# First attention's scores as three products of high and low halves, compressed scores at chunk 37

## The chip, the core and the metric

The kernel runs on one core of a Trainium2 chip. The metric is the device time of one execution in microseconds. The core has a matrix engine (TensorE, PE in the rows; PEld is its loading of weights), a vector engine (VectorE, DVE), an activation engine (ScalarE, ACT), GpSimd (POOL) and SyncE (SP), which here only issues transfers. Each engine works through its own queue in order and waits on semaphores.

## The reference

One decoder layer on 256 tokens of width 2048, all float32. One projection `h @ w_in` of 7704 columns feeds two groups of heads. What the change touches is the scores of the first group: 8 query heads in 2 groups of 4, with compressed, selected and window branches. With 256 tokens the selection and the window keep all past tokens, so both branches are causal attention with their own keys and values.

```python
proj = h @ w_in[l]
...
s = jnp.einsum('bqghd,bngd->bghqn', qc, k_cmp).astype(jnp.float32) * scale
m = cmp_end[None, :] <= t[:, None]
p_cmp = masked_softmax(s, m) * m
o_cmp = jnp.einsum('bghqn,bngd->bqghd', p_cmp.astype(v_cmp.dtype), v_cmp)
...
s = jnp.einsum('bqghd,bgqkd->bghqk', qc, kg).astype(jnp.float32) * scale
p = masked_softmax(s, m)
o_sel = jnp.einsum('bghqk,bgqkd->bqghd', p.astype(vg.dtype), vg)
...
s = jnp.einsum('bqghd,bkgd->bghqk', qc, kwc).astype(jnp.float32) * scale
p = masked_softmax(s, m)
o_win = jnp.einsum('bghqk,bkgd->bqghd', p.astype(vwc.dtype), vwc)
...
o = gc[..., 0:1] * o_cmp + gc[..., 1:2] * o_sel + gc[..., 2:3] * o_win
...
x = x + mixed @ w_out[l]
```

## The kernel before

The weights are a stream of 92 chunks of 128 x 2048 elements, in a fixed order: 60 chunks of the input projection (15 blocks of 512 columns, 4 chunks each), 16 chunks of the first layers that compress keys and values (`ck`, `cv`, 2 at a time among the others up to chunk 39), and 16 chunks of the output projection. All loops run over the chunk number `c`, once on each engine, and what stands in the code for a `c` on one engine stands in that engine's queue in that order. Nothing else sets the order.

A chunk of a projection is split: ACT copies it to `whi` in the type float32r (`split_hi`, L433), DVE subtracts to get `wlo` (`split_lo`, L703), both two such chunks ahead of PE, into 3 buffers. PE multiplies with halves of the activations, also split: high by high, high by low, low by high (L1088 to L1090), 24 products of 512 columns a chunk, 4 k-steps x 2 tiles of 128 tokens x 3. The compressing chunks are 4 float32 products of 32 columns of weights each, and need no split.

Attention runs among the chunks, in units: units 0 to 3 are the first attention (group `u // 2`, branch `1 + u % 2`), units 4 and 5 the second. `UNIT_AT` = 40, 44, 48, 52, 56, 60 is the chunk behind whose products the scores of a unit stand. For unit `u` at chunk `c`:
- PE `scores(u)` behind chunk `c` (L1249): 4 heads, for token tile 0 against 128 keys and for tile 1 against 256, in float32, to the three banks `S`.
- DVE `maxes(u)` and ACT `exps(u)` at `c + 1`, DVE `weights(u)` at `c + 2` (L827 to L834).
- PE `turn_probs(u)` behind chunk `c + 3` (L1266), ACT `take_pT` and DVE `take_pT_lo` (L820) at `c + 4`: high and low halves of the turned probabilities.
- PE `pv_a(u)` behind chunk `c + 4` (L1284 to L1286), three products of halves with 512 moving columns, and where `u` is odd the compressed branch's product (L1296). Unit 4 and 5 have `pv_b` (L1319 to L1321), with 256 moving columns.

The compressed scores `cmp_scores` (L1220, from `qaT` and `kcmpT`, into bank 0 of `S`) stand behind chunk `CMP_SCORES_AT` = 42. One step later DVE masks them, takes the maximum and subtracts it (L978 to L982), ACT takes the exponential at 44 (L650), DVE makes probabilities of it at 45 (L987 to L996), PE turns them behind 46 (L1230), ACT copies them at 47. Rotated queries and keys (`qaT`, `kaT`, `qbT`, `kbT`) are turned by DVE in 16 steps a block (L763), the last of the first attention's (block 4) at chunk 32. `hid` and `vbd` belong to the compressing layers' second half.

## Time and profile before

| what | us |
|---|---|
| runs | 492.05, 493.35, 493.09 (median 493.09) |
| profiled execution, whole | 492.58 |
| its span | 490.8 |
| PE busy | 480.2 |
| PE weight loads busy | 388.8 |
| DVE busy | 357.8 |
| ACT busy | 221.1 |
| POOL busy | 45.7 |

The profiled execution's span is from the first to the last instruction that the profiler saw, and the device time lies 1.8 us above it. Its granted clock of PE is 0.996 of the full one on the mean. In the timelines each product is drawn with its whole duration, longer than the distance to the next, since products are pipelined; the distance from start to start is what one costs. Rows with a count merge instructions of one line that follow one another. A float32 product shows as two instructions, one of the split type as one. Both have `f32` as their type in PE's rows.

### The profile page before, as it was taken

What the parts mean: (1) busy time and instruction counts of PE and PEld (TensorE: products, weight loads), DVE (VectorE), ACT (ScalarE), POOL (GpSimd) and SP (SyncE); (2) the same over time, 40 slices, a digit from 0 to 9 for tenths busy, and PEclk for the clock granted to TensorE, in tenths of its full rate; (3) what the DMA queues carried; (4) which work ended last, traced back from release to release, by engine and by line L of the source; (5) the groups of instructions that cost most, each with busy time, mean ns of one, the idle gap of its engine ahead of it and who ended that gap; (6) DMA issues with size and microseconds to landing.
All of it is one profiled execution on the core that took longest, in us unless ns stands there. A gap on an engine that the chain in (4) does not pass through costs nothing.

```text
span 490.8 us, 6491 instructions
## 1 busy us (share of the span) xinstructions
PE 480.2 (98%) x2554; PEld 388.8 (79%) x2554; DVE 357.8 (73%) x501; ACT 221.1 (45%) x299; POOL 45.7 (9%) x49
## 2 busy tenths in 40 slices
PE   7999999999999999999999999999999999999994
PEld 6878867777777888888888888888888888888883
DVE  4765979368595896999898847488897998444533
ACT  5657423334333365445445454664535443444331
POOL 1002400020201002020020000002000000203050
PEclk9999999999999999999999999999999999999998
DMA  8999958778779434244253425535784454655004
GB/s 275 410 421 419 354 220 315 316 319 308 310 315 391 146 139 160 88 171 172 86 214 130 158 100 183 171 127 206 276 335 171 172 176 180 250 212 210 1 0 172
DMA packets 17725, 107.71 MB, mean 219 GB/s; under 512 B 2208, under 2 KB 2848, under 8 KB 5792
## 3 DMA queue, kind: packets, MB, share of 16 engines
q1 hardware_dynamic: 15968, 103.95, 55.5%
q10 hardware_dynamic: 1728, 3.36, 1.9%
q8 instruction: 20, 0.33, 0.3%
q14 instruction: 9, 0.07, 0.0%
HBM read 105.20 MB, written 2.10 MB: 219 GB/s over the span
## 4 chain that ended last, share of the span: by engine, by line
PE 92%; DMA 4%; DVE 1%; ACT 1%; issue 0%; POOLq 0%; SPq 0%; DVEq 0%; POOL 0%; ACTq 0%
PE acc L1088 27%; PE acc L1090 26%; PE acc L1089 26%; DMA raw<-stream 4%; PE S L1249 3%; PE O L1143 3%; PE S L1266 1%; PE O L1296 1%; PE O L1285 1%; PE O L1286 1%; PE O L1284 1%; DVE wlo L703 0%; ACT whi L433 0%; DVE wlo L726 0%; PE O L1169 0%
## 5 line engine op out<-in xcount | busy, mean ns | idle before, releaser
L703 DVE TENSOR_TENSOR wlo<-raw,whi 128x2048 fp32r<-128x2048 f32 x72 | 165.5, 2303 | 84.2 <-ACT whi L433 83.7
L433 ACT ACTIVATE whi<-raw 128x2048 fp32r<-128x2048 f32 x72 | 137.9, 1917 | 162.0 <-PE acc L1090 149.5
L1088 PE MATMUL acc<-whi,hT_hi 128*128 128x512 f32 x440 | 174.4, 396 | 0.6 <-DVE wlo L703 0.6
L1089 PE MATMUL acc<-wlo,hT_hi 128*128 128x512 f32 x440 | 171.5, 390 | 0.0
L1090 PE MATMUL acc<-whi,hT_lo 128*128 128x512 f32 x440 | 171.4, 390 | 0.0
L1088 PEld LDWEIGHTS acc<-whi,hT_hi 128*128 128x128 f32 x440 | 82.6, 188 | 24.3 <-issue 6.7
L1090 PEld LDWEIGHTS acc<-whi,hT_lo 128*128 128x128 f32 x440 | 82.6, 188 | 17.7
L1089 PEld LDWEIGHTS acc<-wlo,hT_hi 128*128 128x128 f32 x440 | 82.6, 188 | 16.6
L381 POOL TENSOR_TENSOR stage<-stage,stage 128x512 f32<-128x512 f32 (+1 forms) x16 | 23.4, 1476 | 180.9 <-DVE stage L754 180.9
L515 ACT ACTIVATE e<-S,small 128x128 f32<-128x128 f32 (+1 forms) x48 | 19.5, 419 | 26.4 <-DVE small L800 26.4
L763 DVE STREAM_TRANSPOSE zT<-stage 32x256 f32<-32x256 f32 x64 | 27.9, 436 | 2.0
L1088 PE MATMUL acc<-whi,mixA_hi 128*128 128x512 f32 x64 | 24.9, 389 | 0.0
L1089 PE MATMUL acc<-wlo,mixA_hi 128*128 128x512 f32 x64 | 24.9, 389 | 0.0
L1090 PE MATMUL acc<-whi,mixA_lo 128*128 128x512 f32 x64 | 24.9, 389 | 0.0
L1088 PE MATMUL acc<-whi,mixB_hi 128*128 128x512 f32 x60 | 23.3, 389 | 0.0
L1089 PE MATMUL acc<-wlo,mixB_hi 128*128 128x512 f32 x60 | 23.3, 389 | 0.0
L1090 PE MATMUL acc<-whi,mixB_lo 128*128 128x512 f32 x60 | 23.3, 389 | 0.0
L405 POOL TENSOR_TENSOR x_nat<-x_nat,fw 128x512 f32<-128x512 f32 x6 | 11.9, 2003 | 120.9 <-ACT junk L572 120.9
L763 DVE STREAM_TRANSPOSE qaT<-stage 32x256 f32<-32x256 f32 x32 | 14.0, 436 | 3.7 <-POOL stage L381 2.8
L763 DVE STREAM_TRANSPOSE qbT<-stage 32x256 f32<-32x256 f32 x32 | 13.9, 436 | 0.9
L763 DVE STREAM_TRANSPOSE kbT<-stage 32x256 f32<-32x256 f32 x32 | 13.9, 436 | 0.9
L1089 PEld LDWEIGHTS acc<-wlo,mixA_hi 128*128 128x128 f32 x64 | 12.0, 188 | 2.5
(186 smaller groups left out, 487.7 us busy)
## 6 DMA issues: line engine op xcount, KB each, us to landing
raw<-stream SPq DMA_DIRECT2D x72, 1024.0 KB, 4.9
row_raw<-stream SPq DMA_DIRECT2D x16, 1024.0 KB, 6.4
raw<-stream SPq DMA_DIRECT2D x6, 512.0 KB, 9.6
x_nat<-x_rows SPq DMA_DIRECT2D x2, 1024.0 KB, 15.9
x_nat<-x_rows SPq DMA_DIRECT2D x1, 2048.0 KB, 9.3
xTs<-xT SPq DMA_DIRECT2D x3, 512.0 KB, 12.5
raw<-stream SPq DMA_DIRECT2D x4, 256.0 KB, 6.1
fw<-final_w ACTq DMA_DIRECT2D x1, 1024.0 KB, 5.2
```

Source lines behind the costliest of these rows:

```text
L381: pool.tensor_tensor(stage[:, t, 0:w], stage[:, t, 0:w], stage2[:, t, 0:w], ALU.add)\
L405: pool.tensor_tensor(y, y, fw[:, n * NB:(n + 1) * NB], ALU.mult).then_inc(yw_ready, 1)
L433: act.activation(whi[:, n % SPLIT, :], raw[:, n % RAW, :], ACT.Copy).then_inc(hi_ready, 1)
L515: act.activation((e0 if t == 0 else e1)[:, i, :], src, ACT.Exp, bias=nmax[:, 4 * t + i:4 * t + i + 1], accum_out=sums[:, 4 * t + i:4 * t + ...
L703: dve.tensor_tensor(wlo[:, n % SPLIT, :], raw[:, n % RAW, :], whi[:, n % SPLIT, :].bitcast(f32), ALU.subtract)\
L763: dve.transpose(out[:, :, :, SQ * i:SQ * (i + 1)], src[:, :, :, SQ * j:SQ * (j + 1)])\
L1088: pe.matmul(acc_bank(n), xh, wh, start=k == 0, stop=False)
L1089: pe.matmul(acc_bank(n), xh, wl, start=False, stop=False)
L1090: last = pe.matmul(acc_bank(n), xl, wh, start=False, stop=k == KT - 1)
L1143: last = pe.matmul(O[32 * i:32 * (i + 1), k, :], blkf[kind][:, CH * j + i, :, :].rearrange("p g n -> p (g n)"), row_raw[:, m % ROW_RAW, i ...
L1249: last = pe.matmul(dst, q[:, t * P:(t + 1) * P], k[:, 0:w], start=True, stop=True)
L1266: last = pe.transpose(S[:, k, i * P:(i + 1) * P], e[:, i, kt * P:(kt + 1) * P], ident)
```

## The change

- The products of units 0 to 3 are each replaced by three: high by high, high query by low key, low query by high key, all of them float32r. Unit 4 and 5 keep one float32 product.
- The halves are made a group at a time: ACT copies 4 heads of queries (1024 elements a partition) and the group's 2 keys (512) to `q_hi` and `k_hi` (`group_hi`, at c = 38 and 45), DVE subtracts in place to `qa_lo` and `ka_lo` (`group_lo`, at 39 and 46).
- The compressed scores stand behind chunk 37, their mask and shift at 38, their exponential at 39. What follows them stays at 45 to 47.
- `hidT8` moves to another place in memory. Waits are added: unit 0's scores for the mask of the compressed ones and for the low halves, the copy of values of block 9 for the scores of unit 3, the second `hid` for the exponential of the compressed scores, group 1's high halves for the scores of unit 1.

```diff
@@ -75,12 +75,12 @@
 GATE_AT, GATE_TURN = 9, 13
-CMP_SCORES_AT = 42
+CMP_SCORES_AT, CMP_PROBS_AT, HALVES_AT = 37, 45, (38, 45)
 UNIT_AT = [40, 44, 48, 52, 56, 60]
 K_END, V_END = LAST["ck", 0], LAST["cv", 0]
-HID_TURN, KEYS_AT, VALUES_AT = (K_END + 2, CMP_SCORES_AT), K_END + 6, CMP_SCORES_AT + 1
+HID_TURN, KEYS_AT, VALUES_AT = (K_END + 2, V_END + 3), K_END + 6, V_END + 4
 W_PIECES = [(0, i, 1) for i in range(4)] + [(c, i, 2) for c in (1, 2, 3) for i in (0, 2)]
@@ -150,7 +150,9 @@
         hidT = sb("hidT", [P, 4, 2 * NC], at=r1b + 2048)
-        hidT8 = sb("hidT8", [P, 4, 8, NC], at=r1b + 2560)
+        hidT8 = sb("hidT8", [P, 4, 8, NC], at=r1 + 25600)
+        q_hi = sb("q_hi", [P, 4, SEQ], f32r, at=r1 + 16384)
+        k_hi = sb("k_hi", [P, 2, SEQ], f32r, at=r1 + 20480)
         gT = sb("gT", [P, SEQ], at=r1b + 4608)
         kbT = sb("kbT", [P, 8, SEQ], at=r1 + 8192)
@@ -166,6 +168,8 @@
         kaT = sb("kaT", [P, 4, SEQ], at=r2 + 8192)
+        qa_lo = sb("qa_lo", [P, 8, SEQ], f32r, at=r2)
+        ka_lo = sb("ka_lo", [P, 4, SEQ], f32r, at=r2 + 8192)
         va = sb("va_hi", [P, TT, NB], f32r, at=r2 + 12288)
         subw = sb("subw", [P, 2 * HEAD], at=r2 + 15360)
@@ -251,6 +255,7 @@
             sem(n) for n in ("scores_done", "max_ready", "exp_done", "probs_ready"))
+        qk_hi, qk_lo = sem("qk_hi"), sem("qk_lo")
         probs_turned, pT_hi_ready, pT_lo_ready, pv_done, o_taken = (
         cs_done, cs_masked, cs_shift, ce_done, pc_ready, pc_turned, pcT_ready, pc_taken = (
@@ -274,6 +279,10 @@
             return [m[:, t, at] for m in ((va, va_lo) if b == 2 else (vb, vb_lo))]
+
+        def group_keys(m, g):
+
+            return m.rearrange("p (b g) s -> p g b s", g=2)[:, g, :, :]
             kind, b, _ = STREAM[c]
@@ -476,6 +485,8 @@
                 a = use_done(b, t)
+                if b == 9:
+                    act.wait_ge(scores_done, TT * N_A)
                 dst = values(b, t)[0]
@@ -491,6 +502,7 @@
                     act.wait_ge(hid_turned, k)
+                    act.wait_ge(ce_done, 1)
                 act.activation(hid[:, :], O[:, k, :], ACT.Copy).then_inc(hid_taken, 1)
             def silu_hid(k):
@@ -504,6 +516,14 @@
                                        src[:, :, g:g + 1, :].to_broadcast([P, 4, 4, NC]), ACT.Silu).then_inc(hid_act, 1)
+
+            def group_hi(g):
+
+                act.wait_ge(heads_turned, turned(3 + g))
+                if g:
+                    act.wait_ge(scores_done, TT * 2)
+                act.activation(q_hi[:, :, :], qaT[:, 4 * g:4 * g + 4, :], ACT.Copy).then_inc(qk_hi, 1)
+                act.activation(k_hi[:, :, :], group_keys(kaT[:, :, :], g), ACT.Copy).then_inc(qk_hi, 1)
@@ -645,10 +665,13 @@
                     silu_hid(1)
+                for g in range(2):
+                    if c == HALVES_AT[g]:
+                        group_hi(g)
                 if c == CMP_SCORES_AT + 2:
                     act.activation(ce[:, :, :, :], cs[:, :, :, :], ACT.Exp).then_inc(ce_done, 1)
-                if c == CMP_SCORES_AT + 5:
+                if c == CMP_PROBS_AT + 2:
                     act.wait_ge(pc_turned, 1)
                         .then_inc(pcT_ready, 1)
@@ -788,6 +811,15 @@
+            def group_lo(g):
+
+                dve.wait_ge(cs_done, TT)
+                for i, (hi, full, lo) in enumerate(((q_hi[:, :, :], qaT[:, 4 * g:4 * g + 4, :], qa_lo[:, 4 * g:4 * g + 4, :]),
+                                                    (k_hi[:, :, :], group_keys(kaT[:, :, :], g),
+                                                     group_keys(ka_lo[:, :, :], g)))):
+                    dve.wait_ge(qk_hi, 2 * g + i + 1)
+                    dve.tensor_tensor(lo, full, hi.bitcast(f32), ALU.subtract).then_inc(qk_lo, 1)
+
             def maxes(u):
                 for t in range(TT):
@@ -914,6 +946,9 @@
                     turn_z(Z[-1], range(0, 2))
+                for g in range(2):
+                    if c == HALVES_AT[g] + 1:
+                        group_lo(g)
                 if c == VALUES_AT + 1:
                     dve.tensor_tensor(vbd[:, :, :], O[:, 0, P:2 * P].unsqueeze(1).to_broadcast([P, 2, P]),
@@ -981,7 +1016,7 @@
                         .then_inc(cs_shift, 1)
-                if c == CMP_SCORES_AT + 3:
+                if c == CMP_PROBS_AT:
                     cet = ce[:, :, :, :].rearrange("p t h n -> p (t h) n")
                     link(dve.tensor_reduce(cstat[:, 0, :], cet[:, :, 0:N_CMP], AX.X, ALU.add))
@@ -1234,27 +1269,29 @@
                     g, br = unit_a(u)
-                    maps = [(qaT[:, 4 * g + i, :], kaT[:, 2 * (br - 1) + g, :]) for i in range(4)]
+                    kh, kl = k_hi[:, br - 1, :], ka_lo[:, 2 * (br - 1) + g, :]
+                    maps = [((q_hi[:, i, :], kh), (q_hi[:, i, :], kl), (qa_lo[:, 4 * g + i, :], kh)) for i in range(4)]
+                    pe.wait_ge(qk_lo, 2 * (g + 1))
                 else:
-                    maps = [(qbT[:, 4 * m + 2 * (u - N_A) + h, :], kbT[:, 4 * m + 2 * (u - N_A) + h, :])
+                    maps = [((qbT[:, 4 * m + 2 * (u - N_A) + h, :], kbT[:, 4 * m + 2 * (u - N_A) + h, :]),)
                             for m in range(2) for h in range(2)]
                     pe.wait_ge(g_exp, TT)
+                    pe.wait_ge(cs_masked, TT)
                 pe.wait_ge(heads_turned, turned({0: 3, 1: 3, 2: 4, 3: 4}.get(u, 8)))
                     w = (t + 1) * P
-                    for i, (q, k) in enumerate(maps):
+                    for i, terms in enumerate(maps):
                         dst = S[:, 0, i * P:(i + 1) * P] if t == 0 else S[:, 1 + i // 2, (i % 2) * SEQ:(i % 2 + 1) * SEQ]
-                        last = pe.matmul(dst, q[:, t * P:(t + 1) * P], k[:, 0:w], start=True, stop=True)
+                        for n, (q, k) in enumerate(terms):
+                            last = pe.matmul(dst, q[:, t * P:(t + 1) * P], k[:, 0:w], start=n == 0, stop=n == len(terms) - 1)
                     last.then_inc(scores_done, 1)
                 banks_free()
-                if u == 0:
-                    pe.wait_ge(cs_masked, TT)
                 if u == 1:
                 before = sum(8 if v < N_A else 4 for v in range(u))
@@ -1345,7 +1382,7 @@
                     cmp_values()
-                if c == CMP_SCORES_AT + 4:
+                if c == CMP_PROBS_AT + 1:
                     turn_cmp()
                     if c == UNIT_AT[u] + 3:
```

PE behind chunk 37 before (`vblkf` are the two compressing chunks 38 and 39, and behind them stand the products of chunk 40):

```order
L1090 MATMUL acc<-whi,hT_lo 128x512
L1143 MATMUL O<-row_raw,vblkf 32x512 [waits row_in0]
L1143 MATMUL O<-row_raw,vblkf 32x512 x3
L1143 MATMUL O<-row_raw,vblkf 32x512 [waits row_in1]
L1143 MATMUL O<-row_raw,vblkf 32x512 x3
L1088 MATMUL acc<-whi,hT_hi 128x512 [waits acc_read_v,lo_ready,hi_ready]
```

And in the changed kernel:

```order
L1125 MATMUL acc<-whi,hT_lo 128x512
L1255 MATMUL S<-kcmpT,qaT 32x16 [waits heads_turned,kcmp_ready]
L1255 MATMUL S<-kcmpT,qaT 32x16 x63
L1178 MATMUL O<-row_raw,vblkf 32x512 [waits row_in0]
L1178 MATMUL O<-row_raw,vblkf 32x512 x3
L1178 MATMUL O<-row_raw,vblkf 32x512 [waits row_in1]
L1178 MATMUL O<-row_raw,vblkf 32x512 x3
L1123 MATMUL acc<-whi,hT_hi 128x512 [waits acc_read_v,lo_ready,hi_ready]
```

The 64 compressed products stand ahead of the compressing chunks; before, they stand behind chunk 42. Behind chunk 40 each of unit 0's 8 score products became three, with `cs_masked` and `qk_lo` as two more semaphores in the first one's wait.

DVE from the rotation of block 5 (the last `stage` rows) to the scores' maxima of unit 0, before (the first low part is of chunk 42, the second of chunk 43):

```order
L751 SCALAR_TENSOR_TENSOR stage<-acc,const 128x512 [waits heads_turned,acc_done]
L753 SCALAR_TENSOR_TENSOR stage_58<-acc,const 128x4x64
L754 SCALAR_TENSOR_TENSOR stage_58<-acc,const 128x4x64
L703 TENSOR_TENSOR wlo<-raw,whi 128x2048 [waits hi_ready]
L763 STREAM_TRANSPOSE qbT<-stage 32x2x4x32 [waits hid_done,rope_ready]
L763 STREAM_TRANSPOSE qbT<-stage 32x2x4x32 x7
L703 TENSOR_TENSOR wlo<-raw,whi 128x2048 [waits hi_ready]
L799 TENSOR_TENSOR S<-S,const_61 128x512 [waits mask_ready,scores_done]
```

And changed:

```order
L774 SCALAR_TENSOR_TENSOR stage<-acc,const 128x512 [waits heads_turned,acc_done]
L776 SCALAR_TENSOR_TENSOR stage_58<-acc,const 128x4x64
L777 SCALAR_TENSOR_TENSOR stage_58<-acc,const 128x4x64
L1013 TENSOR_TENSOR cs<-S,const 128x128 [waits cs_done]
L1013 TENSOR_TENSOR cs<-S,const 128x128
L1016 TENSOR_REDUCE cstat<-cs 128x16 [waits cs_masked]
L1017 TENSOR_TENSOR cs<-cs,cstat 128x256 [waits vstep]
L821 TENSOR_TENSOR qa_lo<-qaT,q_hi 128x1024 [waits qk_hi,cs_done]
L821 TENSOR_TENSOR ka_lo<-kaT,k_hi 128x2x256 [waits qk_hi]
L726 TENSOR_TENSOR wlo<-raw,whi 128x2048 [waits hi_ready]
L786 STREAM_TRANSPOSE qbT<-stage 32x2x4x32 [waits hid_done,rope_ready]
L786 STREAM_TRANSPOSE qbT<-stage 32x2x4x32 x7
```

The mask and shift of the compressed scores (`cs`) and the two subtractions stand ahead of the low part of chunk 42.

ACT in the same place, before (the second row is the high part of chunk 42):

```order
L433 ACTIVATE whi<-raw 128x2048 [waits chunk_used,raw_in1]
L433 ACTIVATE whi<-raw 128x2048 [waits acc_done,raw_in2]
L494 ACTIVATE hid<-O 128x512 [waits hid_turned,hid_done]
L433 ACTIVATE whi<-raw 128x2048 [waits chunk_used,raw_in3]
L515 ACT_TABLE_LOAD
L515 ACTIVATE e_98,small<-S,small 128x128 [waits max_ready]
```

And changed:

```order
L442 ACTIVATE whi<-raw 128x2048 [waits chunk_used,raw_in1]
L525 ACTIVATE q_hi<-qaT 128x1024 [waits heads_turned]
L526 ACTIVATE k_hi<-kaT 128x512
L673 ACT_TABLE_LOAD
L673 ACTIVATE ce<-cs 128x256 [waits cs_shift]
L442 ACTIVATE whi<-raw 128x2048 [waits acc_done,raw_in2]
L506 ACTIVATE hid<-O 128x512 [waits ce_done,hid_turned,hid_done]
L442 ACTIVATE whi<-raw 128x2048 [waits chunk_used,raw_in3]
L535 ACTIVATE e_102,small<-S,small 128x128 [waits max_ready]
```

The high part of chunk 42 stands behind the two copies and the exponential `ce`, whose table load came from elsewhere: the one ahead of unit 0's exponentials is gone, and one stands now ahead of unit 1's.

DVE from the maxima of unit 1 (`small<-S`) on, before (the low part is of chunk 48, and the rows behind it are the weights of unit 1):

```order
L800 TENSOR_REDUCE small<-S 128x4 [waits vstep]
L763 STREAM_TRANSPOSE kbT<-stage 32x2x4x32 [waits rope_ready]
L763 STREAM_TRANSPOSE kbT<-stage 32x2x4x32 x7
L703 TENSOR_TENSOR wlo<-raw,whi 128x2048 [waits hi_ready]
L827 RECIPROCAL small<-small 128x8 [waits exp_done]
L828 TENSOR_TENSOR small<-small,gate 128x8 [waits vstep]
L834 TENSOR_SCALAR e_98<-e_98,small 128x128 [waits vstep]
L834 TENSOR_SCALAR e_98<-e_98,small 128x128 x3
L834 TENSOR_SCALAR e_99<-e_99,small 128x256 x4
```

And changed:

```order
L832 TENSOR_REDUCE small<-S 128x4 [waits vstep]
L786 STREAM_TRANSPOSE kbT<-stage 32x2x4x32 [waits rope_ready]
L786 STREAM_TRANSPOSE kbT<-stage 32x2x4x32 x7
L821 TENSOR_TENSOR qa_lo<-qaT,q_hi 128x1024 [waits qk_hi,cs_done]
L821 TENSOR_TENSOR ka_lo<-kaT,k_hi 128x2x256 [waits qk_hi]
L726 TENSOR_TENSOR wlo<-raw,whi 128x2048 [waits hi_ready]
L859 RECIPROCAL small<-small 128x8 [waits exp_done]
L860 TENSOR_TENSOR small<-small,gate 128x8 [waits vstep]
L866 TENSOR_SCALAR e_102<-e_102,small 128x128 [waits vstep]
L866 TENSOR_SCALAR e_102<-e_102,small 128x128 x3
L866 TENSOR_SCALAR e_103<-e_103,small 128x256 x4
```

The subtractions of group 1 stand ahead of the low part of chunk 48.

## Rows read from the trace of the kernel before

**Rows 1.** The page: engine busy time (share of the span), and the chain by engine
```profile
PE 480.2 (98%) x2554; PEld 388.8 (79%) x2554; DVE 357.8 (73%) x501; ACT 221.1 (45%) x299; POOL 45.7 (9%) x49
...
PE 92%; DMA 4%; DVE 1%; ACT 1%; issue 0%; POOLq 0%; SPq 0%; DVEq 0%; POOL 0%; ACTq 0%
```

**Rows 2.** Timeline of PE (start us, us, engine, line, work) about unit 0's scores
```profile
164.27 2.78 PE L1249 MATMUL S<-kaT,qaT 128*128 128x128 f32 x16
166.70 0.58 PE L1088 MATMUL acc<-whi,hT_hi 128*128 128x512 f32 x1
167.12 0.40 PE L1089 MATMUL acc<-wlo,hT_hi 128*128 128x512 f32 x1
167.35 0.39 PE L1090 MATMUL acc<-whi,hT_lo 128*128 128x512 f32 x1
```

**Rows 3.** Timeline of PE, products of values in unit 4, 256 moving columns
```profile
306.81 0.28 PE L1319 MATMUL O<-vb_hi,pT_hi 128*128 128x256 f32 x1
306.92 0.28 PE L1320 MATMUL O<-vb_lo,pT_hi 128*128 128x256 f32 x1
...
308.96 1.27 PE L1249 MATMUL S<-kbT,qbT 128*128 128x128 f32 x9
```

**Rows 4.** Groups of PE by form (busy us, mean ns), first attention's scores
```profile
L1249 PE MATMUL S<-kaT,qaT 128*128 128x256 f32 x32 | 7.6, 379 | 0.0
...
L1249 PE MATMUL S<-kaT,qaT 128*128 128x128 f32 x32 | 4.3, 278 | 0.0
```

**Rows 5.** Groups of PE's weight loads by form (busy us, mean ns)
```profile
L1319 PEld LDWEIGHTS O<-vb_hi,pT_hi 128*128 128x128 f32 x12 | 2.3, 191 | 0.1
...
L1143 PEld LDWEIGHTS O<-row_raw,vblkf 128*32 128x32 f32 x64 | 1.9, 109 | 2.9 <-issue 2.9
```

**Rows 6.** Timeline of PE, the compressed scores where they stand before
```profile
178.15 1.33 PE L1220 MATMUL S<-kcmpT,qaT 128*32 128x16 f32 x128
```

**Rows 7.** Timeline of DVE, 158 to 197 us, [idle time before <- released by]
```profile
158.92 2.88 DVE L703 TENSOR_TENSOR wlo<-raw,whi 128x2048 fp32r<-128x2048 f32 x1 [0.63 <-ACT whi L433]
...
178.41 1.92 DVE L834 TENSOR_SCALAR e<-e,small 128x128 f32<-128x128 f32 x8
...
182.46 0.48 DVE L978 TENSOR_TENSOR cs<-S,const 128x128 f32<-128x128 f32 x2
...
183.41 0.42 DVE L982 TENSOR_TENSOR cs<-cs,cstat 128x256 f32<-128x256 f32 x1
...
194.89 2.29 DVE L703 TENSOR_TENSOR wlo<-raw,whi 128x2048 fp32r<-128x2048 f32 x1 [2.67 <-ACT whi L433]
```

**Rows 8.** Timeline of ACT, 151 to 201 us
```profile
151.53 1.92 ACT L433 ACTIVATE whi<-raw 128x2048 fp32r<-128x2048 f32 x1 [5.64 <-PE acc L1090]
156.97 1.92 ACT L433 ACTIVATE whi<-raw 128x2048 fp32r<-128x2048 f32 x1 [3.52 <-PE acc L1090]
...
200.35 0.37 ACT L515 ACTIVATE e<-S,small 128x128 f32<-128x128 f32 x1 [5.49 <-DVE small L800]
```

**Rows 9.** Timeline of DVE, 205 to 236 us
```profile
205.98 2.29 DVE L703 TENSOR_TENSOR wlo<-raw,whi 128x2048 fp32r<-128x2048 f32 x1 [0.20 <-ACT whi L433]
...
208.63 1.92 DVE L834 TENSOR_SCALAR e<-e,small 128x128 f32<-128x128 f32 x8
...
219.06 1.87 DVE L820 TENSOR_TENSOR pT_lo<-S,pT_hi 128x512 fp32r<-128x512 f32 x3
...
235.04 2.29 DVE L703 TENSOR_TENSOR wlo<-raw,whi 128x2048 fp32r<-128x2048 f32 x1 [2.18 <-ACT whi L433]
```

**Rows 10.** Timeline of PE, unit 0's and unit 1's transposes, scores and first value product
```profile
185.88 1.47 PE L1266 MATMUL S<-const,e 128*128 128x128 f32 x12
...
194.72 2.78 PE L1249 MATMUL S<-kaT,qaT 128*128 128x128 f32 x16
...
213.94 1.47 PE L1266 MATMUL S<-const,e 128*128 128x128 f32 x12
...
220.78 0.39 PE L1284 MATMUL O<-pT_hi,va_hi 128*128 128x512 f32 x1
```

## The prediction

> **What bounds the kernel now.** I read the page first: TensorE (PE) is busy for 98% of the span and holds 92% of the chain that ended last, nearly all of it in the three product lines [rows 1]. So a microsecond more or less on PE counts in full, and work on VectorE (DVE) or ScalarE (ACT) counts only where it makes PE wait. Three questions follow, each with its own view: what a score product takes on PE (timeline of PE), how late DVE and ACT may be before PE stands (their timelines beside PE's), and where the delay is caught up.
>
> **PE: the score products.** A unit of the first attention has 8 float32 products, 4 with 128 moving columns and 4 with 256; each shows as two instructions (64 in the trace for four units [rows 4]). In unit 0 they start at 164.27. The product behind them is drawn early and long, so I count back from the one after it, at 167.12, less one pitch of 0.23: 166.89. A unit takes 2.62 us [rows 2], for 4 x (128 + 256) = 1536 columns 1.71 ns a column, four times the 0.43 ns of one pass (below). The other three units are drawn alike.
> The change puts 24 products of high and low halves there: 12 of 256 columns and 12 of 128. For 256 columns there is an exact row: 18 such products run from 306.81 to 308.96, 0.119 each [rows 3]; 12 of them are 1.43 us. For 128 moving columns of this type the trace shows nothing, so the cost is bounded:
> - From below by the slope. 512 columns take 0.23 (167.12 to 167.35 [rows 2]), 256 take 0.119: 0.43 ns a column, so 0.064 for 128. A unit would be 12 x 0.064 + 1.43 = 2.20 us, 0.42 less than now.
> - By the weights. Every product here loads 128 columns of weights anew. A load of 128 columns is drawn at 191 ns and one of 32 at 109 [rows 5], 82 ns for 96 columns, so 128 columns need about 0.109 us of loading however few columns move. The nearest row of the same type has a pitch of 0.119 [rows 3], of which 256 x 0.43 = 0.110 would be the stream alone. With 0.109 a unit is 2.74 us, with 0.119 it is 2.86 us.
> - From above by the rate of float32: 128 columns at 1.71 ns are 0.219, if a narrow moving operand of this type falls back to four passes. A unit would be 4.06 us, 1.44 more than now.
> I take 0.109 to 0.119, since a load of new weights stands before each product and one pass per product is what both other widths of this type show. So a unit takes 0.12 to 0.24 us more, not less, and four take **+0.5 to +1.0**. The saving of a quarter in passes is eaten by the loads: three loads a product instead of two.
> The Trainium skill, TensorE: Matmul & The Clock Gate, section LDWEIGHTS, gives columns divided by 1.2 per ns, 107 ns for 128; by that rule, with which the slope of rows 5 agrees, the sum is the same. Its section Back-to-back issue gap gives about 56 ns for 128 columns where weights don't bind; by that a unit would be 2.10 us and the four would save 2.1. No row here shows such a product.
>
> **PE: compressed scores moved.** 128 instructions of 16 columns take some 1.2 us (1.33 drawn with the last one's end [rows 6]). They go from behind chunk 42 to behind chunk 37, on the same engine, still ahead of everything that reads them: 0 on PE. Their inputs (heads, compressed keys) are turned by chunk 32. The moved block on DVE (mask, maximum, shift) starts at 182.46 and ends at 183.83, 1.4 us, 0.1 of it overlap [rows 7].
>
> **Group 0's halves (chunks 38 to 40).** ACT gets a copy of 1024 and one of 512 elements: 2048 take 1.92 [rows 8], so about 1.5 for both, in the idle time between its work of 151.53 to 153.45 and that of 156.97. DVE gets a subtraction of 1024 and one of 512. 2048 elements take 2.29 (205.98) and 512 about 0.62 (three in 1.87 [rows 9]); between them lie some 1.15 for 1024, 1.75 in all. Their start waits for the shift block. DVE is done with its rotation at 158.29, which is 158.92 less the 0.63 of idle time [rows 7]; the shift block takes it to 159.6, the halves to 161.4. Scores of unit 0 come at 164.27 plus the 1.2 moved ahead of them, 165.5: the halves hide with 4 us to spare. ACT's exponential of the compressed scores now stands ahead of the split of chunk 42, which so starts near 160.0 instead of 156.97; DVE's low part of it ends near 164.2 instead of 161.8. PE wants it a chunk after unit 0's scores, near 173: hidden. Transposes, maxima and weights of unit 0 come about 1.7 later; the weights end at 180.33 before [rows 7], so near 182, and PE turns the probabilities at 185.88 [rows 10]. Hidden. The old place of the shift block gives 1.3 back, and an idle time of 2.67 us ahead of 194.89 [rows 7] takes the rest. So group 0: **0**.
>
> **Group 1's halves (chunks 45 to 46).** ACT's two copies and a table load fall between the end of unit 1's scores (194.72 + 2.62 = 197.3 [rows 10]) and the first exponential at 200.35 [rows 8], whose table was loaded earlier before: 1.5 and 1.3 for the load against 3.0 us, hidden within 0.1. DVE's 1.75 us stand ahead of the low part of chunk 48, which had waited 0.20 [rows 9]: 1.55 of delay. Behind it without idle time are the weights of unit 1, transposes, another low part, the rotation of block 7 and the three low parts of the turned probabilities.
> - The weights end at 210.55; 212.1 then, against PE's turn at 213.94 [rows 9, 10]. Hidden by 1.8.
> - The first low part of the probabilities ends at 219.06 + 0.67 = 219.73, and PE takes it at 220.78 [rows 9, 10]: 1.05 us to spare. With 1.55 of delay PE stands 0.50. The chain on both sides starts from chunk 43 on PE, with one score unit between, so that unit's 0.12 to 0.24 comes off: a stall of 0.25 to 0.4, **+0.3**.
> Later units aren't touched: DVE waits for ACT 2.18 us ahead of 235.04 [rows 9], which absorbs the rest.
> The wait of unit 0 for the masked scores, of the values of block 9 and of the second hidden layer name things done long before; PE's and ACT's queues behind them don't wait.
>
> **Sum.** +0.5 to +1.0 and +0.3, together about +1.0 us. On the profiled execution's own time of 492.58 (span 490.8 and 1.8 around it) that is 493.6; that execution lies 0.5 below the median of the runs, so the forecast on the median of 493.09 is **494.1**. A measurement of this kernel can tell about 0.3% (1.5 us) from no change.
>
> **Rivals.**
> - *Narrow products run at the float32 rate* (the other side, clearly slower). Four times 1.44 is +5.8; PE is then so late at unit 1 that the stall is gone: 498.9. It decides from about 0.13 us per product of 128 columns: there 48 of them, with the 256-column ones, cost 1.4 over the old scores, and 0.1 of stall. For it: the type is stored in 4 bytes like float32, and no product of it in the trace has fewer than 256 moving columns. Against it: 512 and 256 columns lie on one straight line of a single pass.
> - *Loads hide entirely*, 0.064 for 128 columns. The four units save 1.7, but PE then reaches the probabilities of unit 1 0.4 earlier and stands 0.9: net -0.8, 492.3. For it: loads overlap products everywhere. Against it: their slope per column [rows 5]. With the 56 ns of the skill's page named above the units save 2.1 and the stall is near 1.0: 492.0; the page's rule and this rival are the same mechanism, and they share a chance.
> - *The stall is larger*: if ACT's table load and copies push the exponentials of unit 1, or the strided subtraction of the keys is slower than a flat one, by some 1 us, PE stands 1.3 instead of 0.3: 495.1.
> - *The change doesn't do what it says* (the products stay as they were): only the moves and the stall are left, +0.5, 493.6. I give it nothing of its own, since the types are changed in the code.
>
> **How the numbers follow.** My sum 0.48, narrow products at the float32 rate 0.32, loads hidden 0.13, larger stall 0.07. Faster by over 0.3% means under 491.6: only the hidden loads with no stall, 0.05. Slower means over 494.6: the float32 rate, the larger stall, and a sixth of my own case, 0.45. The rest, 0.50, is within 0.3%. The range must reach to the float32 rate, or it leaves out a third: 492.0 to 499.3. The likeliest case alone goes from 493.4 to 494.9.
>
> **What would show it.** Right: the 24 products of a unit take 2.7 to 2.9 us from the first to the next chunk; 256-column ones at 0.119 pitch; PE idle 0.2 to 0.5 us ahead of unit 1's values, released by DVE's low part; no idle time at units 0, 2 and 3. A pitch of 0.22 at 128 columns means the first rival, one of 0.07 the second. Wrong altogether: PE waiting ahead of unit 0's scores, or for a low part of weights after chunk 46.

## The result, and the profile after

| kernel | median, us | runs | profiled whole | span |
|---|---|---|---|---|
| before, beside it | 492.58 (491.97 to 493.35) | 8 | 492.58 | 490.8 |
| changed | 494.89 (493.81 to 495.28) | 8 | 495.08 | 493.2 |

The ratio is 1.0042, with a 95% interval from 1.0032 to 1.0053: 2.1 us slower. It is taken over all runs of both kernels and is not the quotient of the two medians, which lie 2.3 us apart. Runs of one kernel lie 1.4 us apart and more (before: 491.97 to 493.35; in a later group 491.66 to 494.60), so here and below a median can move by half a microsecond and more where the ratio does not. Measured once more beside the last experiment it was 494.92 against 492.97, 1.0038 [1.0024, 1.0051]. The forecast was 494.1, 1.0 us above the median of 493.09 that was known then, with 0.50 on "within 0.3%" and 0.45 on "slower by over 0.3%". So the sign and the range held, but the size was twice what the sum said, and the case with the larger chance was not the one that came. That 494.89 is only 0.8 above the forecast is in part luck: the kernel before, run beside it, had a median 0.5 below 493.09.

The page of the changed kernel, which answers to [rows 1]: busy time of each engine, and the chain that ended last by engine.

```profile
PE 482.0 (98%) x2586; PEld 391.4 (79%) x2586; DVE 361.2 (73%) x505; ACT 224.2 (45%) x303; POOL 45.7 (9%) x49
...
PE 91%; DVE 4%; issue 1%; DMA 1%; ACT 1%; POOLq 0%; DVEq 0%; SPq 0%; POOL 0%; ACTq 0%
```

PE's share of the chain lost a point and DVE's rose from 1% to 4%. So somewhere the chain leaves PE for DVE. How long PE waited there the share does not say: followed back in time, the chain enters DVE at 220.07 and stays in its queue, which had next to no idle time, back to 195.45, while PE was busy beside it. The length of the wait is read from PE's own rows. The timeline of PE (start, us, engine, line, work) about unit 0's scores first, as [rows 2]:

```profile
165.82 0.22 PE L1288 MATMUL S<-k_hi,q_hi 128*128 128x128 f32 x1
165.88 0.28 PE L1288 MATMUL S<-ka_lo,q_hi 128*128 128x128 f32 x1
165.99 0.27 PE L1288 MATMUL S<-k_hi,qa_lo 128*128 128x128 f32 x1
166.10 0.27 PE L1288 MATMUL S<-k_hi,q_hi 128*128 128x128 f32 x1
...
167.28 0.28 PE L1288 MATMUL S<-ka_lo,q_hi 128*128 128x256 f32 x1
167.40 0.28 PE L1288 MATMUL S<-k_hi,qa_lo 128*128 128x256 f32 x1
...
168.60 0.40 PE L1123 MATMUL acc<-whi,hT_hi 128*128 128x512 f32 x1
```

The distance from one start to the next is called the pitch. It is 0.11 us for products of 128 moving columns and 0.12 for those of 256, and the unit takes 168.60 - 165.82 = 2.78 us. The eight float32 products of before took 2.62: 0.16 more a unit, 0.65 for four.

Then the place of the one new stall in PE's timeline that DVE ends (another, of 1.0 us at the start of the program, is in both kernels). Chunk 48's first token tile ends here, and its second begins:

```profile
218.30 0.39 PE L1124 MATMUL acc<-wlo,hT_hi 128*128 128x512 f32 x1
218.53 0.39 PE L1125 MATMUL acc<-whi,hT_lo 128*128 128x512 f32 x1
220.07 0.50 PE L1123 MATMUL acc<-whi,hT_hi 128*128 128x512 f32 x1 [1.16 <-DVE stage L777]
220.41 0.40 PE L1124 MATMUL acc<-wlo,hT_hi 128*128 128x512 f32 x1
```

From 218.53 to 220.07 are 1.54 us where 0.23 is the pitch, and the next step takes 0.34 instead of 0.23: 1.42 us are lost, and the releaser is not `pT_lo` but L777, the last of three operations that rotate a token tile of a finished block. DVE in the changed kernel, as [rows 9]:

```profile
206.38 1.23 DVE L821 TENSOR_TENSOR qa_lo<-qaT,q_hi 128x1024 fp32r<-128x1024 f32 x1
207.52 0.69 DVE L821 TENSOR_TENSOR ka_lo<-kaT,k_hi 128x512 fp32r<-128x512 f32 x1
208.12 2.29 DVE L726 TENSOR_TENSOR wlo<-raw,whi 128x2048 fp32r<-128x2048 f32 x1
...
216.47 2.29 DVE L726 TENSOR_TENSOR wlo<-raw,whi 128x2048 fp32r<-128x2048 f32 x1
218.68 0.68 DVE L774 SCALAR_TENSOR_TENSOR stage<-acc,const 128x512 f32<-128x512 f32 x1
219.28 0.41 DVE L776 SCALAR_TENSOR_TENSOR stage<-acc,const 128x256 f32<-128x256 f32 x1
219.61 0.41 DVE L777 SCALAR_TENSOR_TENSOR stage<-acc,const 128x256 f32<-128x256 f32 x1
...
221.20 1.87 DVE L852 TENSOR_TENSOR pT_lo<-S,pT_hi 128x512 fp32r<-128x512 f32 x3
```

The low part of chunk 48 starts at 208.12 instead of 205.98, and all that follows is 2.14 later. The first rotated tile is ready at 219.61 + 0.41 = 220.02, and PE goes on at 220.07. The second token tile of block 8 accumulates in the bank in which block 7's first tile was kept, and DVE must have read it. The same two places in the trace of before, which stand in no group above, DVE first and then PE:

```profile
217.47 0.41 DVE L754 SCALAR_TENSOR_TENSOR stage<-acc,const 128x256 f32<-128x256 f32 x1
```

```profile
217.80 0.39 PE L1090 MATMUL acc<-whi,hT_lo 128*128 128x512 f32 x1
218.03 0.41 PE L1088 MATMUL acc<-whi,hT_hi 128*128 128x512 f32 x1
```

There DVE let go of the bank at 217.88, and PE wanted it at 218.03. The reserve was 0.15 us, and no wait shows it.

That this accounts for the whole is read from a stretch, from the start of unit 1's transposes to the start of unit 2's scores. Before, the transposes start at 213.94 [rows 10] and the scores at

```profile
224.36 2.89 PE L1249 MATMUL S<-kaT,qaT 128*128 128x128 f32 x16
```

In the changed kernel:

```profile
214.68 1.47 PE L1303 MATMUL S<-const,e 128*128 128x128 f32 x12
...
226.51 0.33 PE L1288 MATMUL S<-k_hi,q_hi 128*128 128x128 f32 x1
```

PE took 10.42 us before and takes 11.83, 1.41 more. With the 0.65 of the products that is 2.06 us, a ratio of 1.0042 on 492.6.

### The profile page after: what moved, and what is told of

It reads as the page before. It is cut to its first block, busy times and chain, and to the rows that moved or that the text cites. A ratio compares the mean times of both kernels' runs of the same rounds, so it can differ in the third digit from the quotient of the medians.

```text
span 493.2 us, 6572 instructions
## 1 busy us (share of the span) xinstructions
PE 482.0 (98%) x2586; PEld 391.4 (79%) x2586; DVE 361.2 (73%) x505; ACT 224.2 (45%) x303; POOL 45.7 (9%) x49
## 4 chain that ended last, share of the span: by engine, by line
PE 91%; DVE 4%; issue 1%; DMA 1%; ACT 1%; POOLq 0%; DVEq 0%; SPq 0%; POOL 0%; ACTq 0%
PE acc L1123 25%; PE acc L1124 25%; PE acc L1125 25%; PE O L1178 3%; PE S L1288 3%; DVE kbT L786 1%; PE acc L1159 1%; PE acc L1166 1%; PE acc L1162 1%; PE S L1303 1%; DMA raw<-stream 1%; DVE wlo L726 1%; PE O L1333 1%; PE O L1322 0%; PE O L1321 0%
## 5 line engine op out<-in xcount | busy, mean ns | idle before, releaser
L1123 PEld LDWEIGHTS acc<-whi,mixA_hi 128*128 128x128 f32 x64 | 12.0, 188 | 2.5
```

The lines of the kernel that those rows point to most:

```text
L1123: pe.matmul(acc_bank(n), xh, wh, start=k == 0, stop=False)
```

## The experiments

Whole times scatter by about 1 us for a reason that lies outside the change, in the first part of the program: two executions of one and the same kernel (`e4_keys_early` and its repeat) start unit 0's scores at 165.75 and 164.80. The middle doesn't scatter: where a kernel was profiled twice, its stretches agree within 0.06 us. So beside each ratio I give starts of PE's rows from the profiled execution: **the middle stretch** (unit 1's transposes to unit 2's scores) and **S1 to S5** (start of unit 1's scores to start of unit 5's). To S1 to S5 the table adds the change of unit 0's own scores; "ratio from it" is 1 plus that sum over 492.6.

| kernel | middle stretch | S1 to S5 | against before, with unit 0 | ratio from it | ratio measured |
|---|---|---|---|---|---|
| before | 10.42 | 114.24 | | | |
| changed | 11.83 | 116.14 | 1.90 + 0.16 | 1.0042 | 1.0042 |
| changed, second time | 11.89 | 116.19 | 1.95 + 0.16 | 1.0043 | 1.0038 |
| moves alone | 10.46 | 114.28 | 0.04 | 1.0001 | 0.9991 |
| group 1's lows late | 10.39 | 114.69 | 0.45 + 0.16 | 1.0012 | 1.0010 |
| halves made, not used | 12.00 | 115.80 | 1.56 | 1.0032 | 1.0037 |
| only query low late | 10.74 | 115.04 | 0.80 + 0.16 | 1.0019 | 1.0035 |
| the same, repeated | 10.71 | 115.01 | 0.77 + 0.16 | 1.0019 | 1.0031 |
| rotation first | 11.07 | 115.36 | 1.12 + 0.16 | 1.0026 | 1.0026 |
| mixed | 10.72 | 113.67 | -0.57 - 0.29 | 0.9983 | 0.9977 |
| mixed, rotation first | 10.38 | 113.35 | -0.89 - 0.29 | 0.9976 | 0.9976 |

### Moves alone: `e1_moves`

```diff
-                for g in range(2):
-                    if c == HALVES_AT[g]:
-                        group_hi(g)
...
-                for g in range(2):
-                    if c == HALVES_AT[g] + 1:
-                        group_lo(g)
...
-                    maps = [((q_hi[:, i, :], kh), (q_hi[:, i, :], kl), (qa_lo[:, 4 * g + i, :], kh)) for i in range(4)]
-                    pe.wait_ge(qk_lo, 2 * (g + 1))
+                    maps = [((qaT[:, 4 * g + i, :], kaT[:, 2 * (br - 1) + g, :]),) for i in range(4)]
```

> Only the moves of the change: compressed scores behind chunk 37, their mask at 38, their exponential at 39; no halves of queries and keys are made and units 0 to 3 keep one float32 product each. Theory A (the +2.3 us are 4 x 0.16 for the products and 1.4 for a stall of PE ahead of the second token tile of chunk 48, where DVE's rotation of block 7 comes too late because group 1's halves stand ahead of it): ratio to the kernel before 1.000, within 0.3 us. Rival B (the moves themselves cost, since unit 0's scores and the exponentials' table load now wait for other things): +0.5 us or more, ratio above 1.001.

492.32 against 492.83 (12 runs), ratio 0.9991 [0.9979, 1.0003], S1 to S5 within 0.04 us of before. The compressed scores five chunks sooner cost nothing and bring nothing.

### Group 1's low halves behind the probabilities: `e2_late`

```diff
-                for g in range(2):
-                    if c == HALVES_AT[g] + 1:
-                        group_lo(g)
+                if c == HALVES_AT[0] + 1:
+                    group_lo(0)
...
+                if c == UNIT_AT[1] + 4:
+                    group_lo(1)
```

> The changed kernel with one edit: DVE makes group 1's low halves behind the low parts of unit 1's turned probabilities (chunk 48) instead of ahead of the low part of chunk 48's weights. Theory A: DVE's rotation of block 7 is back in time, PE doesn't stand at chunk 48, unit 2's scores find their halves ready by about 1.5 us; left are the products, 4 x 0.16 = +0.65 us over the kernel before (ratio 1.0013). Rival C (DVE's 1.75 us only move the stall, to unit 2's scores or the maxima behind them): +1.5 to +2.3 us stay, ratio 1.003 to 1.005.

492.89 against 492.83, ratio 1.0010 [0.9998, 1.0021]. The same products, the same halves, only 1.74 us of DVE's work (206.38 to 208.12 in the changed kernel) in another place, and the middle stretch is 10.39: the whole stall is gone. PE at the token tile where it stood:

```profile
216.93 0.40 PE L1126 MATMUL acc<-whi,hT_lo 128*128 128x512 f32 x1
217.16 0.39 PE L1124 MATMUL acc<-whi,hT_hi 128*128 128x512 f32 x1
217.39 0.39 PE L1125 MATMUL acc<-wlo,hT_hi 128*128 128x512 f32 x1
```

The row at 217.16 is the first of a k-step, and it follows like any other. What stays by the table is 0.61 us, the products.

### Halves made, products as before: `e3_halves_only`

The subtractions write over the high halves here (an edit in `group_lo` that is left out below), and nothing reads the result. The scores are the float32 products of before.

```diff
-                    maps = [((q_hi[:, i, :], kh), (q_hi[:, i, :], kl), (qa_lo[:, 4 * g + i, :], kh)) for i in range(4)]
+                    maps = [((qaT[:, 4 * g + i, :], kaT[:, 2 * (br - 1) + g, :]),) for i in range(4)]
```

> The changed kernel with the old products: the halves of queries and keys are made at the same places (the low ones written over the high ones, so that the full ones stay), but units 0 to 3 take one float32 product each. Nothing reads the halves. Theory A: the stall at chunk 48's second tile is there without any new product, 1.5 us (0.16 more than in the changed kernel, since PE gets there 0.16 sooner), ratio 1.0030. Rival D (the new products make most of the loss, the stall is a coincidence of the profiled run): +0.5 us or less, ratio up to 1.001.

494.73 against 492.83, ratio 1.0037 [1.0025, 1.0049]. PE behind chunk 48's first token tile:

```profile
218.97 0.50 PE L1124 MATMUL acc<-whi,hT_hi 128*128 128x512 f32 x1 [1.33 <-DVE stage L778]
```

The stall comes without a single changed product, and it is 0.17 us longer (1.33 instead of 1.16 of idle time, 12.00 instead of 11.83). That is what a unit of the older products is shorter: PE comes to the bank earlier by that much and waits longer.

### Only the query subtraction late: `e4_keys_early`, `e4b_keys_early`

```diff
-                        group_lo(g)
+                        group_lo(g, (1,) if g else (0, 1))
...
+                if c == UNIT_AT[1] + 4:
+                    group_lo(1, (0,))
```

> The changed kernel with only the subtraction of group 1's queries (1.13 us start to start) moved behind unit 1's low parts; that of its keys (0.6 us) stays ahead of the low part of chunk 48. Theory A, in which the stall is DVE's delay less what it had to spare, about 0.2 to 0.3 us: PE stands about 0.3 at chunk 48's second tile instead of 1.4, total +0.65 + 0.3 = +0.95 us, ratio 1.0019. If the stall is set by something else than the length of DVE's work (a threshold), it stays at 1.4 or is gone: ratio 1.0042 or 1.0013.

> The kernel of the run with group 1's key subtraction alone in its early place, once more, since its profile and its timed runs did not agree: in the profile the stretch from unit 1's turned probabilities to unit 2's scores was 0.32 us longer than before (as expected), which with the products makes +1.0 us, but the timed runs lay 1.8 us above those of the kernel before. If the profile's stretches are the whole of it, the ratio is 1.0019 to 1.0025; if something that the middle of the trace doesn't show belongs to this kernel, it stays at 1.0035.

494.71 against 492.83, 1.0035 [1.0023, 1.0048]; the repeat 494.16 against 492.22, 1.0031 [1.0021, 1.0042]. The place at issue did as expected: 0.61 us of subtraction (start to start) are left in front, less DVE's 0.20 of idle time [rows 9], less 0.16 by which the unit's products bring PE later, less the reserve of 0.15, plus 0.05 from the release to PE's start and 0.11 for the slower step behind a stall, are 0.26, and the stretch is 0.32 and 0.29 longer. PE in the repeat:

```profile
217.51 0.39 PE L1129 MATMUL acc<-whi,hT_lo 128*128 128x512 f32 x1
217.93 0.50 PE L1127 MATMUL acc<-whi,hT_hi 128*128 128x512 f32 x1
```

0.42 where 0.23 is the pitch: a loss of 0.19 that has no idle time printed beside it, which is why distances from start to start are the safer reading. But the whole was 0.6 to 0.8 us above what this place and the products give, both times, and the interval excludes 1.0019 both times. The excess sits at the very end. The last transfer of a result in the repeat, and in before:

```profile
487.29 0.35 ACTq L710 DMA_DIRECT2D result<-x_nat  x1
```

```profile
486.98 0.35 ACTq L687 DMA_DIRECT2D result<-x_nat  x1
```

The spans end at 491.9 and at 490.8, so 4.6 us behind the issue instead of 3.8. The transfer itself is what took longer: from issue to landing

```profile
result<-x_nat ACTq DMA_DIRECT2D x1, 512.0 KB, 4.2
```

in both profiles of this kernel, and 3.3 or 3.4 in before and in every other kernel here. One more packet of instructions was fetched in both profiles (10, elsewhere 9). No run changes that alone, so whether it is the cause stays open.

### The rotation first: `e7_rope_first`

```diff
+                if c == LAST["in", 7]:
+                    take(c, 0)
...
-                take(c, 0)
+                if c != LAST["in", 7]:
+                    take(c, 0)
```

> The changed kernel with one edit on DVE: at chunk 47 the rotation of block 7's first token tile stands ahead of the low part of chunk 49's weights instead of behind it. Theory A (PE at chunk 48 waits for that rotation and nothing else): the stall of 1.4 us there is gone; the same DVE work still stands ahead of unit 1's low parts of the probabilities, so the stall that the prediction named comes out behind it, 0.3 to 0.4 us ahead of unit 1's value products. Total +0.65 + 0.35 = +1.0 us over the kernel before, ratio 1.0020. Rival C (the delay of DVE costs its 1.4 us in whatever place it comes out): ratio 1.0042 as in the changed kernel.

494.30 against 492.22, ratio 1.0026 [1.0013, 1.0039]. DVE frees the bank 2.3 us earlier, so PE passes chunk 48 evenly, and stands at the next thing that DVE is late with, unit 1's first product of values:

```profile
221.05 0.39 PE L1128 MATMUL acc<-whi,hT_lo 128*128 128x512 f32 x1
221.81 0.50 PE L1324 MATMUL O<-pT_hi,va_hi 128*128 128x512 f32 x1 [0.37 <-DVE pT_lo L852]
```

This is the stall that the prediction named, with the releaser that it named. The kernel paid it nowhere, because the larger stall in front of it had made PE late enough. In this order it costs 0.65 us of the middle stretch, more than the 0.3 of the sum. The first `pT_lo` is ready at about 221.74, and PE would have started at 221.28 (221.05 and a pitch): 0.46 late where the sum has 0.25 to 0.4. To that come 0.07 from the release to PE's start and 0.11 for the slower step behind a stall, which the sum left out.

The two medians, 494.30 and 492.22, would give 1.0042 here. The ratio over all runs is the one to read, and the 1.28 us of the table agree with it.

### How wide a moving operand must be: `e5_widths`

This kernel leaves scores out: unit 0 has only 64 keys for the first token tile, unit 2 only 32, unit 4 (float32) 64, and unit 1's second tile has 192.

```diff
-                    w = (t + 1) * P
+                    w = {(0, 0): 64, (1, 1): 192, (2, 0): 32, (4, 0): 64}.get((u, t), (t + 1) * P)
...
-                        dst = S[:, 0, i * P:(i + 1) * P] if t == 0 else S[:, 1 + i // 2, (i % 2) * SEQ:(i % 2 + 1) * SEQ]
+                        dst = S[:, 0, i * P:i * P + w] if t == 0 else S[:, 1 + i // 2, (i % 2) * SEQ:(i % 2) * SEQ + w]
```

> The changed kernel with fewer moving columns in some score products, so that some scores are left out: unit 0's first token tile takes 64 columns instead of 128, unit 2's 32, unit 4's (float32) 64, unit 1's second tile 192 instead of 256. Theory A (a product of 128 columns costs 0.111 us because each loads 128 columns of weights anew): the distance of the narrow products stays at 0.11 us whatever they move, for 64 and 32 columns alike, float32's two instructions of 64 columns too, and at 192 it is 0.11 to 0.12. Rival E (the distance follows the moving columns, with some 0.06 us of fixed cost): 0.085 at 64 columns, 0.07 at 32, 0.095 at 192.

There is one execution of it, 496.68 us, so its time is not compared; its rows are. Products of 64, of 192 and of 32 columns in the timeline of PE:

```profile
165.90 0.28 PE L1288 MATMUL S<-k_hi,qa_lo 128*128 128x64 f32 x1
...
166.91 0.28 PE L1288 MATMUL S<-k_hi,qa_lo 128*128 128x64 f32 x1
...
196.77 0.27 PE L1288 MATMUL S<-k_hi,qa_lo 128*128 128x192 f32 x1
196.88 0.27 PE L1288 MATMUL S<-k_hi,q_hi 128*128 128x192 f32 x1
...
197.10 0.28 PE L1288 MATMUL S<-k_hi,qa_lo 128*128 128x192 f32 x1
...
226.70 0.26 PE L1288 MATMUL S<-k_hi,qa_lo 128*128 128x32 f32 x1
226.81 0.26 PE L1288 MATMUL S<-k_hi,q_hi 128*128 128x32 f32 x1
...
227.70 0.26 PE L1288 MATMUL S<-k_hi,qa_lo 128*128 128x32 f32 x1
```

Nine steps from 226.70 to 227.70 are 0.111 each, nine from 165.90 to 166.91 are 0.112, three from 196.77 to 197.10 are 0.11. So the floor is the same for 32, 64, 128 and 192 columns, and only 256 are above it, at 0.119. What sets the floor does not depend on the moving columns. It is no fixed price of every instruction either: the compressed scores' 128 instructions, with 32 columns of weights each, take 1.33 us together [rows 6]. That the floor is the loading of 128 columns of weights is the reading that [rows 5] gave before, and it fits all four widths; no run varies the columns of weights with this type, so it is argued and not shown. The Trainium skill, TensorE: Matmul & The Clock Gate, section LDWEIGHTS, has 107 ns for such a load, and the pitch in these rows agrees within 5 ns. The 56 ns that the prediction took from its section Back-to-back issue gap, for products where weights don't bind, is met by none of these widths. The same section of the Trainium skill has about 81 ns for a stream of loads and products in pairs, which is nearer to this kernel and which the prediction did not weigh; these rows have 0.111 us in its place.

Unit 4's float32 products did as expected too. With 64 columns for the first token tile the unit starts at 285.57 and PE's second row behind it at 288.53. In the trace of before, with 128 columns, these are 281.60 and 284.56: 2.96 us both times. So a float32 product of 128 columns is already at a floor, two instructions with a load each, and its 0.20 us are not set by its moving columns.

Left-out work did not make the program shorter. Where it got longer the windows show, first of this kernel, then of the changed one (stretch in us, then its length, busy time of PE, PEld, DVE, ACT and POOL with their instructions, the granted clock, DMA share, GB/s):

```profile
226.00:228.50 2.50, 2.50 (x26) 2.38 (x25) 1.92 (x2) 0.00 (x0) 0.00 (x0) 1.00 0.88 279
228.50:232.00 3.50, 3.50 (x14) 3.06 (x13) 2.71 (x4) 1.50 (x8) 0.00 (x0) 0.51 0.95 398
232.00:236.00 4.00, 4.00 (x19) 3.28 (x18) 3.50 (x9) 2.90 (x10) 0.00 (x0) 1.00 0.01 2
```

```profile
228.50:232.00 3.50, 3.50 (x21) 3.05 (x20) 3.35 (x6) 1.93 (x10) 0.00 (x0) 1.00 0.99 407
```

For 3.5 us the granted clock was 0.51, the lower of the two levels (1.2 GHz), and products of 512 columns had a pitch of 0.43 instead of 0.23. Scores of unit 2 to scores of unit 3 took 29.61 us instead of 28.04 in the changed kernel. None of this was in either theory.

### Each width by its cheaper way: `e6_mixed`

A float32 product of 128 columns is two instructions of 0.10 us, 0.20; three products of halves are 0.33. With 256 columns it is 0.45 (2.62 less four times 0.20, over four) against 0.36. So tile 0 keeps float32, tile 1 takes the three products, queries are split for tile 1 alone, and group 1's lows stand late, as in the second experiment.

```diff
+                    whole = [((qaT[:, 4 * g + i, 0:P], kaT[:, 2 * (br - 1) + g, :]),) for i in range(4)]
...
-                act.activation(q_hi[:, :, :], qaT[:, 4 * g:4 * g + 4, :], ACT.Copy).then_inc(qk_hi, 1)
+                act.activation(q_hi[:, :, :], qaT[:, 4 * g:4 * g + 4, P:], ACT.Copy).then_inc(qk_hi, 1)
```

> Same outputs as the changed kernel, another split: units 0 to 3 keep one float32 product per head for the first token tile (128 moving columns) and take three products of halves for the second tile only (256 moving columns). The halves of queries are made for the second tile alone, the low keys go to memory of their own, and group 1's low halves stand on DVE behind unit 1's low parts. Theory A: the first tile costs 4 x 0.22, the second 12 x 0.119, 2.30 us a unit against 2.62 before: -0.32 each, -1.3 us; PE then comes 0.3 sooner to chunk 48's second tile, where the rotation of block 7 had some 0.15 to spare: a stall of about 0.15. In all -1.1 us, ratio 0.9977. Rival E (mixing the two types costs at the turns, or PE waits elsewhere): 0 to -0.5 us, ratio 0.999 or above.

491.29 against 492.22, ratio 0.9977 [0.9964, 0.9990]. Unit 0 on PE:

```profile
164.85 1.05 PE L1291 MATMUL S<-kaT,qaT 128*128 128x128 f32 x8
165.66 0.36 PE L1291 MATMUL S<-k_hi,q_hi 128*128 128x256 f32 x1
165.86 0.28 PE L1291 MATMUL S<-k_lo,q_hi 128*128 128x256 f32 x1
...
167.18 0.40 PE L1124 MATMUL acc<-whi,hT_hi 128*128 128x512 f32 x1
```

0.81 and 1.52 us, together 2.33 instead of 2.62 or 2.78. It is faster than both kernels. In chunk 48 it still lost 0.3 us at the second token tile, since PE now comes there earlier:

```profile
216.67 0.39 PE L1126 MATMUL acc<-whi,hT_lo 128*128 128x512 f32 x1
217.09 0.50 PE L1124 MATMUL acc<-whi,hT_hi 128*128 128x512 f32 x1
```

That is 0.19 above the pitch and 0.11 for the slower step behind it, the 0.30 by which its middle stretch is above that of before.

### Mixed, rotation first: `e8_mixed_rope`

The kernel above with the edit of `e7_rope_first`.

> The mixed version (first token tile of each unit in float32, second in three products, group 1's low halves late) with the rotation of block 7's first tile taken ahead of the low part of chunk 49. The mixed version still lost about 0.2 us at the second token tile behind chunk 48. Theory A: the rotation's early place takes these 0.2 us back, and VectorE has room enough for unit 1's pT_lo behind it; the profiled middle stretch falls by 0.2 us against the mixed version and the whole is about 0.9973 of before. Rival: VectorE has no room, the 0.2 us come out again as idle time ahead of unit 1's value products, as 0.37 us did in the changed kernel with this order, and the ratio stays 0.9977.

491.84 against 492.97, ratio 0.9976 [0.9963, 0.9988]. The middle stretch is 10.38, 0.34 less than in the mixed kernel, so that place is clean: DVE's `pT_lo` starts at 218.25, and PE's first product of values follows at 219.58 with an even pitch. The whole does not tell it from the mixed kernel; the intervals cover each other, and 0.34 us is under what the runs resolve. So the choice between theory A's 0.9973 and the rival's 0.9977 rests on the stretch alone.

The changed kernel was run again beside it:

> The changed kernel as it is, a second time, beside the mixed version on the same chip: the sum of narrow products (0.65 us) and the stall behind chunk 48 (1.41 us) gives 1.0042 again. Rival: the start of the program, which takes up to 1.2 us more or less from one execution to the next, made part of the first result, and the ratio comes nearer to 1.003.

1.0038 [1.0024, 1.0051], between the two values expected and telling neither apart. Its trace has the same stall, 1.17 us of idle time released by L777, and the same S1 to S5 within 0.05.

## Why the prediction was right or wrong

The forecast's range held, but not by its mechanism. The term of the score products was right. The term of the stall named a wait that the changed kernel never had, and missed the one that it had. The range reached far enough only because of a rival that did not come: the likeliest case alone, 493.4 to 494.9 on a median of 493.09, does not contain 1.0042 times that median, 495.2.

- **What bounds the kernel.** Held. Every difference found is time of PE, by longer products or by one wait.
- **Score products, 0.12 to 0.24 a unit, 0.5 to 1.0 in all.** Held: 0.16 a unit, 0.65. Of the three bounds for 128 columns the weights' one was the right one (0.109 to 0.119; 0.111 came). The changed kernel's own rows exclude the slope of 0.43 ns a column (0.064) and the float32 rate (0.22), and `e5_widths` shows that fewer columns don't lower the pitch. The reading of float32 as 1.71 ns a column throughout was an average: 128 columns take 0.20 us and 256 take 0.45.
- **Compressed scores moved, 0.** Held, by `e1_moves`.
- **Group 0's halves, 0.** Held in the changed kernel's trace: no idle time of PE at unit 0, and DVE is done with the halves at 162.13, 3.7 us ahead of unit 0's scores at 165.82. In the table all that is lost lies in the products and in group 1's halves on DVE.
- **Group 1's halves on ACT, "hidden within 0.1".** The first exponential of unit 1 moved from 200.35 [rows 8] to 201.22. In this execution PE came to unit 1's scores 0.56 later (195.28, [rows 10] have 194.72) and took 0.16 longer for them; the copies and the table load took the rest. DVE didn't wait for it, so it cost nothing.
- **Group 1's halves on DVE, 0.3.** This is the step that failed. Its sign, PE idle for 0.2 to 0.5 us ahead of unit 1's values, did not come: the first of them starts at 222.92, a pitch behind the product ahead of it at 222.70. The prediction listed who waits for DVE behind the low part of chunk 48: the weights, then "the first low part of the probabilities", with 1.05 us to spare. Between the two stands the rotation of block 7, which it named as work in the queue and not as a release of an accumulator bank. PE needs that bank for the second token tile of chunk 48, with 0.15 to spare. The size of the delay was right: 1.55 less a unit's 0.16 is 1.39, and DVE's 2.14 less the 0.73 by which PE itself was later (218.30 against 217.57 for the same product) is 1.41. Less the reserve of 0.15, plus 0.05 from the release to the start and 0.11 for the slower step behind it, that is 1.42 lost, and 1.41 is the stretch. `e2_late` takes it away, `e3_halves_only` has it without the new products, `e4_keys_early` scales it with the length of what stands in front, and `e7_rope_first` turns it into the stall that was forecast.
- **"The chain on both sides starts from chunk 43", so the products' own cost comes off.** Right in kind: in `e3_halves_only`, where the products are the older ones, the stall is 0.17 longer.
- **"Later units aren't touched."** Held: unit 2's scores to unit 3's take 28.04 instead of 27.90, and unit 3's to unit 4's 29.51 instead of 29.34, about a unit's 0.16 each.
- **Rivals.** The float32 rate had 0.32 and did not come; its evidence (4 bytes, no narrow example) was weak beside two widths on one line, and it pulled the range up to 499.3. The range's lower end, 492.0, comes from 56 ns a product of 128 columns, and no row of this case shows such a pitch. The "larger stall" had 0.07 and was nearest in size (495.1), but by another mechanism: not a late exponential, a bank.
- **Two slips in the working.** 48 products at 0.13 us with the 256-column ones cost 1.5 over the old scores, not 1.4 (6.24 + 5.72 - 10.48). And the chances named for "slower", 0.32, 0.07 and a sixth of 0.48, add up to 0.47, not 0.45. Neither changes the forecast.

So the sum would have been 0.65 + 1.41 = 2.06, and the forecast 495.15 on the median of 493.09, had the queue been followed instruction by instruction to every engine that waits for it.

## What to carry to other kernels

When work is put into a queue, go through all that stands behind it until the next idle time, and ask of each instruction what it releases: not only its result, also the buffer or bank that it reads for the last time. A wait that is met 0.15 us early showed no idle time in any view here, so reserves have to be worked out by setting the end of the release beside the start of the work that needs it. Splitting a float32 product into three single-pass ones paid here with 256 moving columns (0.36 us against 0.45) and not with 128 (0.33 against 0.20), which fits three loads of new weights against two, if the load is what sets the floor; and the halves should be made where DVE has idle time behind them.

## What the runs showed of the hardware

- A product of this type with new weights of 128 columns does not start more often than every 0.111 us, whether 32, 64, 128 or 192 columns move. With 256 it is 0.119, with 512 0.23. A unit of float32 products takes 2.96 us to PE's second row behind it with 64 columns in the first tile as with 128.
- The first product behind a stall takes 0.34 us to the next where 0.23 is the pitch (the changed kernel at 220.07, and the same in `e3_halves_only`, `e4b_keys_early` and `e6_mixed`).
- Twelve products of 32 columns, 1.36 us of them, and five of 256, with PE drawn as busy all the time, stood ahead of 3.5 us at a granted clock of 0.51. In the changed kernel, whose unit 2 has 128 columns there, the clock stays at 1.00 in the same windows. It stayed at 1.00 too behind the 64-column products of unit 0, and in before behind the compressed scores, 1.33 us of instructions with 16 moving columns each. This is one place in one execution, and what exactly lets the clock fall is not shown.
- The last transfer of a result, 512 KB, took 4.2 us to land in both profiles of `e4_keys_early` and 3.3 to 3.4 in all others, so that this kernel's program ended 4.6 us behind the issue instead of 3.7 to 3.8. That is 0.16% of the time, the edit is elsewhere in the program, and the cause stays open.
